# Two fused layers: the embedding projection moved to the boundary between the layers, copied out by ScalarE and kept in DRAM

## What is computed

```python
def first_block(x, ...):               # proj = h @ w_in, recurrent and convolution mixers
    ...
    m = jax.nn.sigmoid(g_a) * y_a + jax.nn.sigmoid(g_b) * y_b
    o = m @ w_out[l]
    x = x + gate * rms_norm(o, post_gain[l])

def second_block(x, p, ...):
    hn = rms_norm_2(h, norm_mix[i])
    h = h + nsa_mixer(hn, ...)         # attention
    hn = rms_norm_2(h, norm_ffn[i])
    h = h + jnp.square(jax.nn.relu(hn @ ffn_w1[i])) @ ffn_w2[i]
    gate = jax.nn.sigmoid(rms_norm_2(h, norm_ple[i]) @ ple_w_gate[i])
    h = h + (p[i] @ ple_w_proj[i]) * gate
    return rms_norm_2(h, norm_final)
```

## Time and profile before

| | us |
|---|---|
| median of 3 runs | 2300.02 (2299.59 to 2300.27) |
| profiled execution, its own time | 2300.34 |
| its span in the profile | 2298.8 |
| TensorE matmul busy | 2218.6, 97% |
| VectorE busy | 1552.4, 68% |
| ScalarE busy | 1106.5, 48% |
| GpSimd busy | 131.0, 6% |
| granted TensorE clock, mean | 0.99 |

### The profile page before, as it was taken

One profiled execution on the slowest core, in us unless ns is written; L12 is line 12 of the kernel. 1 busy time (PEld: TensorE's weight loads), 2 busy tenths in 40 slices (PEclk: granted clock), 3 DMA queues, 4 the chain that ended last, 5 costly groups with the idle time before them and its releaser, 6 DMA issues.

```text
span 2298.8 us, 40482 instructions
## 1 busy us (share of the span) xinstructions
PE 2218.6 (97%) x15116; PEld 1868.5 (81%) x15116; DVE 1552.4 (68%) x2342; ACT 1106.5 (48%) x1745; POOL 131.0 (6%) x128
## 2 busy tenths in 40 slices
PE   6999999999999999989999999999999999999997
PEld 3688887888888888868888878788888888888785
DVE  6768776767776568577666667765565565566766
ACT  2344454555544465454455445444454444445553
POOL 0011000000000010110000002100000000001213
PEclk9999999999999999999999999999999999999998
DMA  9989643333334476635543435455555555555542
GB/s 391 378 312 343 242 142 119 128 128 131 128 121 138 155 233 226 202 126 175 188 138 128 135 127 179 157 196 188 185 181 189 187 183 186 179 192 182 171 158 73
DMA packets 114685, 420.63 MB, mean 183 GB/s; under 512 B 13088, under 2 KB 13216, under 8 KB 114304
## 3 DMA queue, kind: packets, MB, share of 16 engines
q1 hardware_dynamic: 106848, 390.68, 49.6%
q0 software_dynamic: 7712, 28.19, 3.4%
HBM read 412.52 MB, written 6.29 MB: 182 GB/s over the span
## 4 chain that ended last, share of the span: by engine, by line
PE 86%; DVE 8%; ACT 3%; DMA 2%; issue 2%; DVEq 0%; SPq 0%; ACTq 0%
PE ps L2043 46%; PE ps L2044 23%; PE ps L2161 5%; PE ps L2423 3%; DVE wlo L1221 1%; PE ps L2424 1%; DMA raw<-in_stream 1%; ACT whi L688 1%; DVE acts L1232 1%; PE ps L2555 1%; DVE acc L1252 1%; PE ps L2096 1%; PE ps L2097 0%; PE ps L2098 0%; DMA xt<-in_x 0%
## 5 line engine op out<-in xcount | busy, mean ns | idle before, releaser
L2043 PE MATMUL ps<-acts,whi 128*128 128x512 f32 x3520 | 1283.8, 407 | 25.3 <-DVE wlo L1221 6.5
L1221 DVE TENSOR_TENSOR wlo<-raw,whi 128x1024 fp32r<-128x1024 f32 x647 | 812.2, 1265 | 611.5 <-ACT whi L688 609.7
L688 ACT ACTIVATE whi<-raw 128x1024 fp32r<-128x1024 f32 x671 | 704.0, 1058 | 736.6 <-PE ps L2044 658.0
L2044 PE MATMUL ps<-acts,wlo 128*128 128x256 f32 x3520 | 988.7, 281 | 0.0
L2043 PEld LDWEIGHTS ps<-acts,whi 128*128 128x128 f32 x3520 | 664.3, 189 | 199.6 <-issue 22.4
L2044 PEld LDWEIGHTS ps<-acts,wlo 128*128 128x128 f32 x3520 | 668.3, 190 | 4.5 <-issue 3.4
L2043 PE MATMUL ps<-hidn,whi 128*128 128x512 f32 x1280 | 453.5, 399 | 2.3 <-DVE s L1227 1.8
L2044 PE MATMUL ps<-hidn,wlo 128*128 128x256 f32 x1280 | 358.1, 280 | 0.0
L2043 PEld LDWEIGHTS ps<-hidn,whi 128*128 128x128 f32 x1280 | 240.1, 188 | 64.9 <-DVE s L1227 4.0
L2044 PEld LDWEIGHTS ps<-hidn,wlo 128*128 128x128 f32 x1280 | 241.5, 189 | 0.5 <-issue 0.5
L688 ACT ACTIVATE half<-ps 128x256 f32<-128x256 f32 (+1 forms) x361 | 135.8, 386 | 91.7 <-PE ps L2044 59.2
(11 more groups left out here) (323 smaller groups left out, 1957.6 us busy)
## 6 DMA issues: line engine op xcount, KB each, us to landing
raw<-in_stream SPq DMA_DIRECT2D x735, 512.0 KB, 3.9
graw<-in_ada_gate POOLq DMA_DIRECT2D x32, 512.0 KB, 5.5
gate_dram<-stage POOLq DMA_DIRECT2D x32, 128.0 KB, 2.6
gab<-gate_dram POOLq DMA_DIRECT2D x8, 512.0 KB, 5.1
xt<-in_x SPq DMA_DIRECT2D x1, 2048.0 KB, 9.7
xt<-in_x POOLq DMA_DIRECT2D x1, 2048.0 KB, 9.2
out<-y__142 SPq DMA_DIRECT2D x4, 512.0 KB, 2.8
con<-in_con SPq DMA_DIRECT2D x1, 898.0 KB, 4.9
```

The lines of the kernel that those rows point to most:

```text
L688: return nc.scalar.activation(dst, src, ACT.Copy)
L1221: tt(wlo[:, n % SPLIT, :], raw[:, g % RAW, :], whi[:, n % SPLIT, :].bitcast(F32), ALU.subtract).then_inc(raw_used, 1)
L2043: mm(ps[bank + n][:, :], whi[:, n0 % SPLIT, c:c + P], act[:, off + kt + k, :], start=kt + k == 0, stop=False)
L2044: ins = mm(ps[bank + n][:, 0:T], wlo[:, n0 % SPLIT, c:c + P], act[:, off + kt + k, 0:T], start=False, stop=kt + k == last)
```

## The change

The four tiles `PR0` move in the stream from behind the feed-forward to between `WO0` and `NS0`. The embedding is loaded into a place of its own before the third gate load of layer one's end, and split into `pes` before the output projection. TensorE computes the projection right after the output projection. It uses three matmuls of 256 columns (high by high, high by low, low by high) in place of a 512 and a 256, so that a bank holds two complete output tiles; the order of banks is `PR_BANKS`. ScalarE alone copies each bank into `pr_` (128x512), and no addition is needed. GpSimd stores `pr_` in DRAM in four parts (`ple_dram`), and loads it back into `pj` after the attention. The sums of squares stand behind the projection's first tile. In the norm at the boundary each pair of `xt` tiles is now followed by the split of one weight tile, on both engines. In the gate block `last_split(3)` stands behind the second (ScalarE) and third (VectorE) weight split of the first block, and the sum of squares before its seventh tile instead of its sixth.

```diff
@@ -40,2 +40,3 @@
 RAW, SPLIT = 8, 4
+PR_BANKS = (5, 6, 7, 0, 1, 2, 5, 6)
 CW = 1024
@@ -56,3 +57,4 @@
 WO0 = PAB0 + 4 * 8
-NS0 = WO0 + 4 * 8
+PR0 = WO0 + 4 * 8
+NS0 = PR0 + 4
 GT0 = NS0 + 2 * 8
...
@@ -187,3 +189,3 @@
         stream += [blocks(w1[:, f * D:(f + 1) * D]), blocks(w2[f * D:(f + 1) * D])]
-    stream += [blocks(i["ple_w_proj_2"][0]), blocks(i["ple_w_gate_2"][0])]
+    stream.append(blocks(i["ple_w_gate_2"][0]))
     stream = np.concatenate(stream, 0)
@@ -335,2 +337,4 @@
         lora, a = sb("lora", [P, DA], a)
+        pe_, _ = sb("pe_", [P, 2, T], a - 4 * DA)
+        pes, _ = sb("pes", [P, 2, 2 * T], a - 2 * DA, F32R)
         stage, a = sb("stage", [P, 8, T], a)
...
@@ -658,2 +665,3 @@
                     gp.wait_ge(s.pool_moved, 64 * HT + 16)
+                    gp.dma_start(pe_[:, :, :], ple_in).then_inc(s.ple_in, 16)
                 if b >= 2:
@@ -667,2 +675,6 @@
             squares(evac_done, [33 + 8 * HT + 32 + 4 * (q + 1) for q in range(3)], ob, 1, sqa, sqt, 3)
+            for b in range(4):
+                gp.wait_ge(s.pr_out, 2 * b + 2)
+                gp.dma_start(ple_dram[4 * b:4 * b + 4, :, :].rearrange("a p t -> p a t"), pr_[:, 4 * b:4 * b + 4, :]
+                             ).then_inc(s.ple_out, 16)
             gp.wait_ge(s.ss_ps, 3)
@@ -675,3 +687,4 @@
             gp.wait_ge(s.attn_done, 2 * GQ)
-            gp.dma_start(pe_[:, :, :], ple_in).then_inc(s.ple_in, 16)
+            gp.wait_ge(s.ple_out, 64)
+            gp.dma_start(pj[:, :, :], ple_dram[:, :, :].rearrange("a p t -> p a t")).then_inc(s.ple_again, 16)
             squares(s.res_done, [4, 8, 12, 16], xt, 3, sqb, squ, order=(1, 0, 2, 3))
@@ -954,2 +967,4 @@
                     copy(acts[:, 4 * b + n, 0:T], m4[:, n, :]).then_inc(s.m_hi, 1)
+            act.wait_ge(s.ple_in, 16)
+            copy(pes[:, :, 0:T], pe_[:, :, :]).then_inc(s.pes_hi, 1)
@@ -961,5 +976,11 @@
             tile_squares(evac_done, E + 32 + 12, ob, sql)
+            split(PR0 + AHEAD)
             rms(1)
-            E0 = E + 32 + KT + 4 * NG + 4
+            def projected(x):
+                act.wait_ge(quarters, used(PR0 + x // 2) - 2 + x % 2 * 2)
+                copy(pr_[:, 2 * x:2 * x + 2, :], ps[PR_BANKS[x]][:, :].rearrange("p (a t) -> p a t", a=2)).then_inc(s.pr_out, 1)
+
+            projected(0)
+            projected(1)
@@ -968,3 +989,3 @@
                     split(g0 + j + AHEAD, i)
-                    if j == 7 and use != 2:
+                    if j == 7:
                         rms(use)
@@ -973,5 +994,12 @@
-            for c in range(KT):
-                scaled_hi(s.x_done1, c // 2 + 1, xt, vec[:, V_MIX:V_MIX + KT], c)
-                nc.scalar.activation(sqx[:, c, :], xt[:, c, :], ACT.Square).then_inc(s.tile_sq, 1)
+            for q in range(8):
+                split(NS0 + q)
+                if q < 3:
+                    projected(2 * q + 2)
+                    projected(2 * q + 3)
+                for c in (2 * q, 2 * q + 1):
+                    scaled_hi(s.x_done1, q + 1, xt, vec[:, V_MIX:V_MIX + KT], c)
+                for c in (2 * q, 2 * q + 1):
+                    nc.scalar.activation(sqx[:, c, :], xt[:, c, :], ACT.Square).then_inc(s.tile_sq, 1)
+
             def tile(j):
@@ -997,3 +1025,5 @@
-            first_block(NS0, 2)
+            for j in range(5, 8):
+                tile(j)
+            halves(7)
             tile(8)
...
@@ -1129,4 +1160,2 @@
             no_split(3)
-            act.wait_ge(s.ple_in, 16)
-            copy(pes[:, :, 0:T], pe_[:, :, :]).then_inc(s.pes_hi, 1)
@@ -1174,10 +1203,2 @@
-            for b in range(4):
-                split(PR0 + b + AHEAD)
-                for n in range(4):
-                    act.wait_ge(evac_done, E0 + 9 * KT + 4 * b - 4 + n + 1)
-                    second_half(n, PR0 + b, bank=n + b % 2 * 4)
-                if b == 0:
-                    last_split(3)
-
             def final_gain(b):
@@ -1192,2 +1213,4 @@
                         split(PG0 + j + AHEAD, b)
+                    if first and j == 1:
+                        last_split(3)
                     if first and j == 7:
@@ -1637,2 +1660,4 @@
                        ).then_inc(s.m_done, 1)
+            dve.wait_ge(s.pes_hi, 1)
+            tt(pes[:, :, T:2 * T], pe_[:, :, :], pes[:, :, 0:T].bitcast(F32), ALU.subtract).then_inc(s.pes_lo, 1)
@@ -1651,13 +1677,11 @@
             gain = vec[:, V_MIX:V_MIX + KT]
-            for q in range(9):
-                if q < 8:
-                    v = slice(2 * q, 2 * q + 2)
-                    for c in range(2 * q, 2 * q + 2):
-                        V.do(stt(ob[:, c, :], ob[:, c, :], gpost[:, c:c + 1], rs[:, :], ALU.mult, ALU.mult))
-                    V.wait()
-                    tt(xt[:, v, :], xt[:, v, :], ob[:, v, :], ALU.add).then_inc(s.x_done1, 1)
-                if q:
-
-                    for c in range(2 * q - 2, 2 * q):
-                        scaled_lo(1, xt, gain, c)
+            for q in range(8):
+                v = slice(2 * q, 2 * q + 2)
+                for c in (2 * q, 2 * q + 1):
+                    V.do(stt(ob[:, c, :], ob[:, c, :], gpost[:, c:c + 1], rs[:, :], ALU.mult, ALU.mult))
+                V.wait()
+                tt(xt[:, v, :], xt[:, v, :], ob[:, v, :], ALU.add).then_inc(s.x_done1, 1)
+                split(NS0 + q)
+                for c in (2 * q, 2 * q + 1):
+                    scaled_lo(1, xt, gain, c)
@@ -1668,2 +1692,4 @@
                         split(g0 + j + AHEAD, b)
+                    if j == 2 and first is not None:
+                        last_split(3)
                     if j == 7 and first is not None:
@@ -1711,3 +1737,3 @@
-            for j in range(8):
+            for j in range(5, 8):
                 tile(j)
@@ -1932,4 +1958,2 @@
             E += KT
-            dve.wait_ge(s.pes_hi, 1)
-            tt(pes[:, :, T:2 * T], pe_[:, :, :], pes[:, :, 0:T].bitcast(F32), ALU.subtract).then_inc(s.pes_lo, 1)
@@ -1995,10 +2019,2 @@
-            for b in range(4):
-                split(PR0 + b + AHEAD)
-                for n in range(4):
-                    first_half(pj[:, 4 * b + n, :], n, E + 4 * b + n, bank=n + b % 2 * 4)
-                if b == 0:
-                    last_split(3)
-            E += KT
-
             def ple_gate(b, last, first=None):
...
@@ -2432,4 +2449,23 @@
             E += 16
-            square_sum(1, sqa, sql, 0)
+            pe.wait_ge(s.pes_lo, 1)
+            for b in range(4):
+                n0 = (PR0 + b - WA0) % SPLIT
+                pe.wait_ge(raw_used, RAW + PR0 + b + 1)
+                for n in range(4):
+                    bank = PR_BANKS[2 * b + n // 2]
+                    if n % 2 == 0 and bank < 4:
+                        pe.wait_ge(evac_done, E - 4 + bank + 1)
+                    elif n % 2 == 0 and b == 3:
+                        pe.wait_ge(s.pr_out, n // 2 + 1)
+                    dst = ps[bank][:, n % 2 * T:(n % 2 + 1) * T]
+                    for k in range(2):
+                        c = k * 512 + n * P
+                        mm(dst, whi[:, n0, c:c + P], pes[:, k, 0:T], start=k == 0, stop=False)
+                        mm(dst, whi[:, n0, c:c + P], pes[:, k, T:2 * T], start=False, stop=False)
+                        ins = mm(dst, wlo[:, n0, c:c + P], pes[:, k, 0:T], start=False, stop=k == 1)
+                    ins.then_inc(quarters, 1)
+                if b == 0:
+                    square_sum(1, sqa, sql, 0)
+            pe.wait_ge(s.pr_out, 6)
             for j in range(8):
@@ -2628,7 +2664,3 @@
-            pe.wait_ge(s.pes_lo, 1)
-            for b in range(4):
-                use(PR0 + b, act=pes, last=1, bank=b % 2 * 4, evac=(E + 4 * b, -4 if b == 0 else -8))
-            E += KT
-            first_block(PG0, 3, 0, (E - 4, 0), sqb, 3, acts, 5)
+            first_block(PG0, 3, 0, (E - 4, 0), sqb, 3, acts, 6)
             with pe.Fori(1, 4) as b:
```

15 lines of the change are left out of this document (10 added, 5 removed).

## The result

The change takes **2276.75 us** (median of 4 runs, 2275.43 to 2278.92), before 2300.14 us (4 runs): ratio 0.9903, 95% interval 0.9888 to 0.9917, some 22 to 23 us less. The forecast was 2277.6. The profiled execution took 2277.07 us, its span is 2275.5.

A forecast was written before the change was run, and what follows sets the result against it. TensorE works nearly all the time, so only its gaps can be won back. 2.9 + 1.1 + 18.4 = 22.4 us off the profiled 2300.34 gives 2277.9, 0.3 above the median: forecast 2277.6 us, range 2273.0 to 2284.5.

The forecast's parts named there:

- Tail, -16.74: Embedding projection near the end: its four tiles leave, so the gate block starts where the projection started, 16.74 us less.
- Clock fall at the gate's start, -1.65: Start of the gate block: TensorE's clock should stay up once the waits on the projection's evacuations go, 1.65 us less.
- The fall behind the first gate block: After the first gate block: clock fall may or may not recur; left in, 1.65 us kept for the range's lower end.
- Boundary, -2.9: Between the layers: the projection fills TensorE's gap and the first block ends 2.9 us earlier; bounds 1.8 and 5.7.
- the sums: At the boundary: five sums of squares behind the first projection tile cost 2.3 us; bounds 2.0 and 2.9.
- Start of the output projection, 0: First layer: an added ScalarE copy and VectorE low half cost nothing, with 0.6 us of cover; otherwise up to 1.2.
- Feed-forward start, -1.1: Without `pes` the weight halves start 1.21 us earlier, so the 2.29 us wait becomes about 1.1; bounds nothing and 2.3.
- the wait on `wlo` at the feed-forward is near 1.1 us: Feed-forward start: a sign that the forecast is right, TensorE's wait for weight halves being near 1.1 us.
- Rival A: Boundary stalls again: waits add 0.5 us a pair, TensorE waits with a clock fall, 5.6 us, 2283.2; chance 0.12.
- Rival B: Gate block: GpSimd holds the weight halves, 2.8 us wait and 1.65 clock fall, 2282.0; chance 0.05.
- Rival C: No clock fall after first gate block (1.65), boundary's eight tiles at 3.5 us (1.5): 2274.4; chance 0.08.
- Rivals D and E: D: clock falls under the boundary's short matmuls, 2310.6, chance 0.03. E: boundary and tail waits persist, about 2297, chance 0.03.

The follow-up runs named there:

- order_tail: Kernel before, with only the last four scaled activations of the gate block moved behind its second and third weight split; 2296.32 us, ratio 0.9975.
- norm_old: The change, with the boundary norm's weight splits for NS0 + 3 to NS0 + 7 back behind all the pairs; 2291.9 us, ratio 0.9952.
- order_both: Kernel before, with the new split order at the boundary and in the gate block, the projection still in the tail; 2288.45 us, ratio 0.9938.
- tail_old: The change, with the last four scaled activations back ahead of the gate block's first weight split, on both engines; 2279.39 us, ratio 0.9913.
- root_early: The change, with root and reciprocal two weight splits earlier in the first feed-forward and gate blocks, TensorE's sums one tile earlier; 2271.25 us, ratio 0.9874.

## Why the prediction was right, and where it was not

- **Tail, -16.74.** Exact. The gate block started straight behind the feed-forward, and the last four activations, at 2170.52 to 2173.71, were ready 4.3 us before the tile at 2178.06 that needs them. Forecast were 3.7 us of cover. Two errors cancelled here: held weight halves let the activations start later than forecast, and they were done 12.6 us behind the start of the gate block, forecast 12.9.
- **Clock fall at the gate's start, -1.65.** It went: the first gate block took 24.68 us instead of 26.35. Gate and end took 2.6 us less; the other 0.8 lie behind the landing of the last output store, which comes 14.8 us behind the start of the last sums of squares in both. The span ended 1.2 us after it in all four kernels with the projection in the tail, and 0.3 to 0.4 us after it in all ten that have it at the boundary. Nothing in the forecast stood for this, and its cause stays open. The fall behind the first gate block, which the forecast left in as uncertain, came five pairs long in both kernels (that block took 24.39 us before and 24.37 after), and not at all in the change's second profile, where gate and end took 4.1 us less.
- **Boundary, -2.9.** Measured -3.4, between 42.82 and 42.84 us in all eight profiles of kernels that keep the change's boundary. Of its pieces, the 96 matmuls took 2.82 + 8.74 = 11.56 us (forecast 11.5), the sums 1.97 (forecast 2.3, bounds 2.0 and 2.9), eight tiles 29.31 (29.5). The first pair was there 11.1 us behind the start of the boundary, forecast 11.1. The last copy that frees one of the banks 0 to 2 ended at 1009.1, 0.9 us before TensorE wanted them; forecast 1.1. The one term outside its bounds is the sums, by 0.03 us.
- **Start of the output projection, 0.** Right: TensorE has no wait there in either trace. The low half of the embedding took 0.68 us, not 1.2. VectorE of the kernel after:

```profile
911.64 0.68 DVE L1662 TENSOR_TENSOR pes<-pe__105,pes 128x512 fp32r<-128x512 f32 x1
912.34 3.49 DVE L1244 TENSOR_TENSOR wlo<-raw,whi 128x1024 fp32r<-128x1024 f32 x3
```

- **Feed-forward start, -1.1.** This step failed: the wait went from 2.29 to 1.85 us, 0.44. "Without `pes` the weight halves start 1.21 us earlier" was true, and "VectorE runs without a pause there" was read as "VectorE runs at its own pace". It did not. VectorE and GpSimd of the kernel after:

```profile
1431.63 6.49 DVE L1255 SCALAR_TENSOR_TENSOR acts<-xt,vec,acts 128x256 fp32r<-128x256 f32 x4
1438.05 5.15 DVE L1244 TENSOR_TENSOR wlo<-raw,whi 128x1024 fp32r<-128x1024 f32 x4
```

```profile
1437.92 0.79 POOL L635 TENSOR_TENSOR sqb<-sqb 128x256 f32<-128x256 f32 x1
```

Four weight halves took 5.15 us here and 4.62 in the kernel before (at 1444.57), where `pes` stood ahead of them and took the hold instead: it needed 1.21 us, and 0.68 where GpSimd was still. Counted from the end of GpSimd's squares (1438.71 here, 1444.11 before) TensorE goes on 1.23 us later here and 1.82 before: 0.59 us, about the free length of `pes`, and not the 1.21 that the row shows. The wait shrank by less still, since TensorE's first three tiles were 0.16 us faster here. The sign "the wait on `wlo` at the feed-forward is near 1.1 us" was missed.
- **Rival A** (the boundary stalls): its condition, 0.5 us more a pair, did not arise; 3.46 us a pair were less than the 3.6 assumed.
- **Rival B** (GpSimd holds the weight halves): I gave as evidence against it that no weight half was long beside GpSimd's squares. That was no evidence: in the kernel before GpSimd squared from 2167.43 to 2175.02 there, and the weight halves of that stretch started at 2167.19 and 2175.22, none of them beside it. In the change they stand beside it and are held. VectorE of the kernel after:

```profile
2165.30 1.95 DVE L1244 TENSOR_TENSOR wlo<-raw,whi 128x1024 fp32r<-128x1024 f32 x1 [0.88 <-ACT whi L701]
2168.07 2.52 DVE L1244 TENSOR_TENSOR wlo<-raw,whi 128x1024 fp32r<-128x1024 f32 x1 [0.82 <-ACT whi L701]
2170.52 3.19 DVE L1255 SCALAR_TENSOR_TENSOR acts<-xt,vec,acts 128x256 fp32r<-128x256 f32 x4
```

The same lengths stood in the trace before, ahead of the feed-forward (1.95 and 2.53 us at 1416.57 and 1419.35); that stretch I had not read. The mechanism was real, and its price zero: the halves were 0.7 and 1.3 us late out of a lead of three tiles. The evacuation of a bank beside GpSimd's squares is not held: four took 1.41 us at 2175.16 in order_tail, with GpSimd busy from 2174.24 to 2177.50. This agrees with the Trainium skill, "SBUF — State Buffer", section "Who interferes with whom", which counts a VectorE instruction's inputs in SBUF: a weight half has two, an evacuation one, the other being in PSUM.
- **Rival C** (more is won) came half true: the boundary's eight tiles took 3.66 us each, not 3.5, and the fall behind the first gate block was missing in one of two profiles.
- **Rivals D and E** fell: the granted clock was 1.00 under the short matmuls, and no gap took the old one's place.

**Luck.** That the median came within 0.9 us of the forecast is in part luck. Against the forecast the profile of the change has 2.1 us less in the opening, 0.9 less in gate and end and 0.5 less at the boundary, and 2.5 more in the feed-forward. The opening's part and the clock fall in the feed-forward come and go between executions of the same code, and the 0.8 us at the very end was in no term.

What my account lacked is the split between order and place: some 13 of 22 us were to be had without moving the projection.

## What to carry to other kernels

When an engine at 97% waits for a norm, look for work that depends on nothing and stands in a place where it is paid in full; here 12.5 us of it cost 3.2 in the gap, and its results could go through DRAM at no cost that was measured. Do it together with the order of the helpers' work: splits between the pairs, not behind all of them, or the gap only moves (10.57 us in norm_old). And when an instruction is to be removed or put elsewhere, compare its length with that of the same form where GpSimd is idle first: a VectorE instruction with both inputs in SBUF that stands beside GpSimd's squares has a length that is not its own. A wait put on GpSimd's queue moves those squares onto whatever VectorE does later.

## What was not expected of the hardware

**Two paces at full clock.** Windows of 100 us of the same feed-forward code at the granted clock of 1.00 hold different numbers of matmuls. One window of order_both, and the same one of tail_old:

```profile
1600.00:1700.00 100.00, 100.00 (x564) 86.00 (x563) 61.38 (x92) 46.47 (x63) 0.00 (x0) 1.00 0.55 187
```

```profile
1600.00:1700.00 100.00, 100.00 (x570) 86.53 (x569) 62.32 (x92) 46.55 (x64) 0.00 (x0) 1.00 0.56 187
```

In the timelines a pair of matmuls takes 0.346 or 0.353 us, for whole blocks of eight tiles at a time, and changes from one to the other at the start of a block. The feed-forward took 728.4 to 737.8 us in the eleven profiles whose kernels have the same code there (but for `pes`, in four of them). Their waits in it differ by 0.8 us at most, and a fall of the clock, of which they have none to two, is worth 1.5; some 6 us of the 9.4 are left for the pace. That is of the size of the spread of single runs (2293 to 2302 us for the kernel before on one chip); that it is the cause of that spread is not shown, since most kernels have only one profile. It is why a term of 1 us is better read from a single wait than from a median. What sets the pace stays open; no run was made on it.

**The clock behind a gap of about 2 us.** In one profile of the change it was 0.50 behind the wait of 2.47 us at 1456.95 (the window above). In the other one, the same kernel and the same wait, of 2.42 us at 1461.28, the clock stayed:

```profile
1461.00:1464.00 3.00, 2.72 (x15) 2.42 (x16) 3.00 (x10) 0.08 (x1) 0.00 (x0) 1.00 0.10 38
```

Behind the waits of 4.1 us and more at the boundary it fell in every profile that has them. It also fell behind waits of 1.76 to 1.91 us at the gate block, in some of them only when TensorE had done three or four pairs after the wait, and in other profiles it stayed at 1.00 behind a wait of the same length there. A fall costs 1.2 to 1.7 us (four to six pairs at 0.64 us instead of 0.35), so the two short waits that root_early removes are worth 4.3 us when the clock holds and 7.3 when it does not.
